# The heads of two mixers' attention passed in one row, one step apart on each engine, and queries and keys turned in banks of their own

## The reference, cut to what matters

```
h = rms_norm(x, mix_norm[l])
(na_q, na_k, na_v, df_q, df_k, df_v,
 gq_q, gq_k, gq_v, dl_q, dl_k, dl_v) = split_in_proj(h @ w_in[l])
o_a = neighborhood_attention(...)      # 4 heads of 64, with a bias
o_b = diff_attention(...)              # 4 heads, each two softmaxes of width 32, p[0] - lam*p[1]
o_c = gqa_axial_attention(...)         # 4 query heads, 2 key/value heads of 64
o_d = dilated_attention(...)           # 4 heads of 64, log-counts as a bias
o = jnp.concatenate([o_a, o_b, o_c, o_d], axis=-1)
x = x + o @ w_out[l]
```

## Time and profile before

| | |
|---|---|
| median of 3 runs | 3191.75 us (3189.97 to 3192.04) |
| the profiled execution, its time | 3195.57 us |
| the profiled execution, its span | 3193.5 us |
| PE busy | 3029.3 us, 95% of the span |
| DVE busy, ACT busy, POOL busy | 2097.6 us, 1597.0 us, 492.8 us |
| mean granted clock of PE | 0.974 |
| the chain that ended last | PE 85%, DVE 10%, ACT 3% |
| the two mixers | about 2245 to 2413 us and 2822 to 2989 us of the span |

### The profile page before, as it was taken

One profiled execution on the slowest core, in us unless ns is written; L12 is line 12 of the kernel. 1 busy time (PEld: TensorE's weight loads), 2 busy tenths in 40 slices (PEclk: granted clock), 3 DMA queues, 4 the chain that ended last, 5 costly groups with the idle time before them and its releaser, 6 DMA issues.

```text
span 3193.5 us, 56060 instructions
## 1 busy us (share of the span) xinstructions
PE 3029.3 (95%) x21820; PEld 2730.7 (86%) x21820; DVE 2097.6 (66%) x4342; ACT 1597.0 (50%) x3039; POOL 492.8 (15%) x371
## 2 busy tenths in 40 slices
PE   8989999999998989999999999799979999998899
PEld 8789999988787879999988888699768989976798
DVE  4559988799655456987879945654665455456544
ACT  5445544444555545554444455455535555553454
POOL 1213210000021112320000022222101213210121
PEclk9999999999999999999999999899989999999999
DMA  6345554444554334554445555455314556542354
GB/s 213 119 146 170 180 166 159 160 161 164 187 192 160 127 122 160 171 173 158 159 159 166 166 198 195 171 187 180 126 59 149 190 181 197 185 141 70 113 188 155
DMA packets 139512, 512.60 MB, mean 161 GB/s; under 512 B 15713, under 2 KB 16242, under 8 KB 137970
## 3 DMA queue, kind: packets, MB, share of 16 engines
q1 hardware_dynamic: 134352, 489.22, 46.6%
q10 hardware_dynamic: 4898, 19.81, 1.7%
HBM read 507.92 MB, written 1.05 MB: 159 GB/s over the span
## 4 chain that ended last, share of the span: by engine, by line
PE 85%; DVE 10%; ACT 3%; issue 1%; DMA 1%; ACTq 0%; DVEq 0%; SPq 0%
PE ps L415 84%; DVE WL L1580 2%; ACT WH L1037 1%; PE ps L419 1%; ACT BIG L1133 1%; DVE BIG L1692 1%; DVE BIG L1741 1%; DMA RAW<-in_w 0%; DVE XTl L1619 0%; DVE BIG L1655 0%; DVE H L1658 0%; DVE BIG L2025 0%; DVE BIG L1986 0%; DVE BIG L2032 0%; DVE BIG L1633 0%
## 5 line engine op out<-in xcount | busy, mean ns | idle before, releaser
L1037 ACT ACTIVATE WH<-RAW 128x512 fp32r<-128x512 f32 x1866 | 1168.5, 630 | 1193.8 <-PE ps L415 1167.1
L1580 DVE TENSOR_TENSOR WL<-RAW,WH 128x512 fp32r<-128x512 f32 x1537 | 1109.7, 725 | 868.6 <-ACT WH L1037 860.7
L415 PE MATMUL ps<-XTh,WH 128*128 128x256 f32 x3928 | 1131.6, 288 | 22.4 <-DVE XTl L1788 8.2
L415 PE MATMUL ps<-XTl,WH 128*128 128x256 f32 x3928 | 1120.6, 285 | 0.0
L415 PE MATMUL ps<-XTh,WL 128*128 128x256 f32 x3928 | 1119.9, 285 | 0.0
L2309 POOL TENSOR_TENSOR WL<-RAW,WH 128x512 fp32r<-128x512 f32 x329 | 441.3, 1341 | 2652.8 <-ACT WH L1037 2652.8
L415 PEld LDWEIGHTS ps<-XTh,WH 128*128 128x128 f32 x3928 | 762.9, 194 | 34.1 <-DVE WL L1580 14.5
L415 PEld LDWEIGHTS ps<-XTl,WH 128*128 128x128 f32 x3928 | 763.5, 194 | 3.1
L415 PEld LDWEIGHTS ps<-XTh,WL 128*128 128x128 f32 x3928 | 762.8, 194 | 0.0
L415 PE MATMUL ps<-WH,GH 128*128 128x512 f32 x1408 | 562.5, 399 | 20.0 <-DVE GL L2100 8.1
L415 PE MATMUL ps<-WL,GH 128*128 128x512 f32 x1408 | 554.0, 393 | 0.0
(11 more groups left out here) (182 smaller groups left out, 2209.3 us busy)
## 6 DMA issues: line engine op xcount, KB each, us to landing
RAW<-in_w SPq DMA_DIRECT2D x933, 512.0 KB, 3.3
BIG<-in_ln ACTq DMA_DIRECT2D x4, 1024.0 KB, 6.3
GAIN<-in_norms ACTq DMA_DIRECT2D x6, 512.0 KB, 4.1
BIG<-in_sk ACTq DMA_DIRECT2D x2, 1024.0 KB, 5.0
BIG<-in_na_bias ACTq DMA_DIRECT2D x2, 1024.0 KB, 10.2
BIG<-in_qk_gain ACTq DMA_DIRECT2D x2, 960.0 KB, 6.6
BIG<-in_memT ACTq DMA_DIRECT2D x4, 256.0 KB, 7.6
BIG<-in_xT ACTq DMA_DIRECT2D x1, 1024.0 KB, 5.5
```

The costliest lines, as they stand in the source:

```text
L415: return self.e.matmul(out, lhsT, rhs, start=start, stop=stop, skip_group_check=loose)
L1037: e.activation(wh, raw, ACT.Copy).then_inc(*c.hi.mark(j))
L1580: e.tensor_tensor(wl, raw, wh.bitcast(F32), ALU.subtract).then_inc(*c.lo_v.mark(j))
```

## The change

Three things are changed. First, the row of heads: `march` hands out, at every step, which head is new on PE and which are one, two, three and four steps old, over all 20 heads of a mixer in one row, without an end between groups; a group's head enters only when its queries, keys and values are there. On PE a step is now the turn of the head two steps old, then the scores of the new one, and after a yield the values of the head three steps old. DVE and ACT do maximum and exponentials of the head that is one step old, the copy of the turned head after the yield, and the division of the head four steps old. A step costs 1.4 + 0.9 where it cost 0.9 + 0.5 + 0.9 before. Second, one set of attention buffers serves all groups. Third, queries and keys are turned in banks 0/1 (`na`, `df`), 2/3 (`gq`) and, as before, 6/7 (`dl`), and the output pair of `na` goes to bank 0. Both memory attentions use the same row with one group.

```
+QK_BANK = {"na": 0, "df": 0, "gq": 2, "dl": 6}
-ATT_STEPS = {"scores": 0.9, "turn": 0.5, "values": 0.9}
+ATT = (1.4, 0.9)
...
-        t.att = [self.att_views(Arena(big, ar.at + 3700 * k)) for k in range(2)]
+        t.att = self.att_views(ar)
...
+def march(pace, groups):
+    ids = [(g, i) for g in groups for i in range(len(g.heads))]
+    flow, n = [None] * 4, 0
+    while n < len(ids) or any(x is not None for x in flow[-4:]):
+        enters = n < len(ids) and ids[n][0].needs <= pace.reached
+        flow.append(n if enters else None)
+        n += enters
+        at = flow[:-6:-1]
+        if all(x is None for x in at):
+            flow.pop()
+            yield None
+            continue
+        yield at
+        if at[4] is not None:
+            g, i = ids[at[4]]
+            if i == len(g.heads) - 1:
+                pace.reached.add(g.tag)
...
 class Tensor
+    def attention(self, groups, t):
+        for at in march(self.pace, groups):
+            ...
+            new, _, turn, out, _ = at
+            if turn is not None:
+                ps = self.bank(6)
+                for blk in range(2):
+                    e.wait_ge(*c.exps.at(*ids[turn], blk))
+                    ...
+                self.empty[6] = (c.probs_a if turn % 2 else c.probs_v).at(*ids[turn])
+            if new is not None:
+                h, ps = heads[new], self.bank(4 + new % 2)
+                ...
+            yield ATT[0]
+            if out is not None:
+                e.wait_ge(*(c.probs_a if out % 2 else c.probs_v).at(*ids[out]))
+                ps = self.bank(7)
+                ...
+                self.empty[7] = c.att_out.at(*ids[out])
+            yield ATT[1]
...
 class Tensor, norm
-            b = 6 + (g // 2) % 2
+            b = QK_BANK[name] + (g // 2) % 2
 class Tensor, first_out_mix
-        self.pair(stage, c.mix.O, 0, 6, [c.att_out.at((stage, "na"), 3)])
+        self.pair(stage, c.mix.O, 0, 0, [c.att_out.at((stage, "na"), 3)])
 class Tensor, Scalar and Vector, mix_stage
-        pace.bg += [self.attend(stage, name, k % 2) for k, name in enumerate(NAMES)]
+        pace.bg.append(self.attention(c.mix_groups(stage), t.att))
...
 class Scalar
+            _, n, turn, _, _ = at
+            if n is not None:
+                if n >= 3:
+                    e.wait_ge(*c.flipped.at(*ids[n - 3]))
+                e.wait_ge(*c.maxed.at(*ids[n]))
+                (two exponentials)
+            yield ATT[0]
+            if turn is not None and turn % 2:
+                (copy of the turned head)
+            yield ATT[1]
...
 class Vector
+            _, n, turn, _, done = at
+            if n is not None:
+                (bias, maximum)
+            if done is not None:
+                (division)
+            yield ATT[0]
+            if turn is not None and turn % 2 == 0:
+                (copy of the turned head)
+            yield ATT[1]
```

More of the change, by code:

```diff
@@ L318, in mem_heads, with mix_groups @@
         return heads
+    def mix_groups(self, stage):
+        return [Group((stage, name), self.mix_heads(name), [(stage, "made", name), (stage, "v", name)]) for name in NAMES]
     def mix_heads(self, name):
@@ L347, in __init__, with flat @@
         self.q, self.k, self.v, self.col, self.bias, self.minus = q, k, v, col, bias, minus
[L350 to L358, removed]
+class Group:
+    def __init__(self, tag, heads, needs=()):
+        self.tag, self.heads, self.needs = tag, heads, set(needs)
+def march(pace, groups):
[15 more added lines that the diff above has]
+                pace.reached.add(g.tag)
+def flat(groups):
+    return [h for g in groups for h in g.heads], [(g.tag, i) for g in groups for i in range(len(g.heads))]
 def top_steps(n, cost):
@@ L539, in pair @@
         self.empty[b] = c.xtl.at(stage, "o", g)
[L541 to L545, removed]
+    def attention(self, groups, t):
+        c, e = self.c, self.e
+        heads, ids = flat(groups)
+        for at in march(self.pace, groups):
+            if at is None:
+                yield 1.0
+                continue
+            new, _, turn, out, _ = at
[3 more added lines that the diff above has]
+                    e.wait_ge(*c.exps.at(*ids[turn], blk))
+                    for k in range(2):
+                        m = self.tr(ps[:, k * 256 + blk * 128:k * 256 + blk * 128 + 128],
+                                    t.E[:, turn % 3, blk * 256 + k * 128:blk * 256 + k * 128 + 128])
+                m.then_inc(*c.flipped.mark(*ids[turn]))
+                self.empty[6] = (c.probs_a if turn % 2 else c.probs_v).at(*ids[turn])
+            if new is not None:
+                if ids[new][1] == 0:
+                    self.ready(*ids[new][0])
+                h, ps = heads[new], self.bank(4 + new % 2)
@@ L2327, in inner, with attention @@
             yield cost
-    def attention(self, tag, n):
-        yield from att_steps(n)
-        self.pace.reached.add(tag)
+    def attention(self, groups):
+        for at in march(self.pace, groups):
+            if at is None:
+                yield 1.0
+                continue
+            yield ATT[0]
+            yield ATT[1]
     def states(self):
@@ L2483, in norm @@
         self.pace.reached.add((stage, "made", name))
-    def attend(self, stage, name):
-        while not {(stage, "made", name), (stage, "v", name)} <= self.pace.reached:
-            yield 1.0
-        yield from self.attention((stage, name), 8 if name == "df" else 4)
     def mix_stage(self, layer):
@@ L2496, in mix_stage @@
         pace.reached |= {(stage, "v", "na"), (stage, "v", "df")}
-        pace.bg += [self.attend(stage, name) for name in NAMES]
+        pace.bg.append(self.attention(self.c.mix_groups(stage)))
         self.halves(8)
```

195 lines of the change are left out of this document (75 added, 120 removed).

## The result

The changed kernel takes 3206.78 us (median of 6 runs, 3200.34 to 3208.52) against 3191.89 (median of 6, 3188.70 to 3194.04): 1.0045 of the time before, 95% interval 1.0032 to 1.0058. It is slower, by 14 to 15 us, where 3183 was forecast and 3194 was the top of the range.

What follows compares the result with a forecast made beforehand. PE was taken to bound the mixers: waits plus clock loss go from 28.4 to 22.8 us a mixer, less 1 for hand-overs, so 4.6 each, 9.2 for two. From the median 3191.75 that gives 3183 us, range 3171 to 3194.

Steps and rivals of the forecast that it cites:

- the hand-overs: Mixers: 1 us a mixer taken off the gain for hand-overs between engines that the step-by-step count leaves out.
- The bound and the two sums: Mixers' attention: PE bounds; 20.7 us idle and 7.9 us of clock, together 28.4 a mixer, are the most to win.
- The memory attentions: Two memory attentions, same row with one group: waits few and apart, so no effect, within 1 us each way.
- The removed waits: Mixers: nearly all of 20.5 us of PE's waits go, among them 2.87 on the pair's low part and 3.5 before the second pair.
- The added waits: Mixers: new PE waits, mostly behind norms and divisions on DVE, eight over 1.3 us, 18.8 us a mixer in all.
- the walk: Mixers: PE, DVE and ACT followed through the new order with traced durations, giving 18.8 us of waits against 20.5.
- The 0.7 us of the held operation: `gq` norm on DVE: a small operation takes 0.91 us, not 0.17, under POOL's low part; 0.7 of the 3.5 us wait.
- I take 2 each, 4 a mixer, against 7.9: Clock in the mixers: two low spells instead of three, costing 2 us each, 4 a mixer where it was 7.9.
- the prediction's own sign of being wrong: Profile after: wrong if low spells are four or more, waits on copies are small, or waits appear in feed-forward stages.
- Waits only moved: Rival, mixers: the clock still loses 7.9, so only 0.7 us a mixer is won; 3190 (3187 to 3194), chance 0.27.
- Slower: Rival, mixers: eight waits over 1.3 us, five low spells of 2.6 us, 4.4 us a mixer lost; 3200, chance 0.11.
- Wrong if waits on copies are small (then the gain is twice as large): Sign, mixers: small waits on copies would mean DVE keeps further ahead than assumed, doubling the gain.

Runs made afterwards that it cites:

- m1_mem_cost: The changed kernel, but in the two memory attentions a step charges the pace only for what it does, 9.2 in all instead of 18.4: 3197.23 us, ratio 1.0008.
- m3_banks_only: The kernel before with the bank change alone (turned queries and keys, first output pair): 3193.28 us, ratio 1.0006.
- m7_before_fill: The kernel before with 14, 9 and 20 matmuls of no use at its mixers' waits of 2.60, 1.75 and 3.55 us: 3193.00 us, ratio 0.9997.
- m14_before_act_copies: The kernel before with all copies of turned heads in the mixers on ACT: 3195.24 us, ratio 1.0010.
- m11_divide_first: The changed kernel with the memory price mended, all turned heads in the mixers copied by ACT, and DVE's division ahead of the maximum: 3196.57 us, ratio 1.0013.
- m6_fill_all: The changed kernel with the memory price mended and 19, 14, 8 and 11 matmuls of no use at PE's waits in each mixer: 3182.78 us, ratio 0.9962.

## Why the prediction was wrong, point by point

In the traces the forecast of -9.2 us became +12.1. The account in us, forecast against measured, with the clock by the windows of 2 us:

| term, whole kernel | forecast | measured | off by |
|---|---|---|---|
| two memory attentions | 0 | +9.3 | +9.3 |
| clock in the two mixers | -7.8 | +13.6 | +21.4 |
| PE's idle time in them, with the hand-overs | -1.4 | -15.3 | -13.9 |
| the rest of PE's longer work in them | 0 | +5.1 | +5.1 |
| elsewhere | 0 | -0.6 | -0.6 |

So the clock was the largest miss, and the error in the idle time hid more than half of it: that the mixers came out only 12.6 us off is luck.

**The bound and the two sums.** Right that PE bounds the mixers and that idle time and clock can be won or lost: filling the idle time on PE moved the kernel from 3197 to 3183 with its order as it was. Wrong in "no instruction is added or dropped, so the sum is one of waits": the matmuls are the same, but no two heads' scores run together any more, and PE's work grew by some 2.5 us a mixer beyond the clock. The sum had no term for that.

**The memory attentions, "I take nothing, within 1 us each way".** The first step that failed: 9.5 us by m1_mem_cost, three quarters of the 12.1 in the trace, and so most of the loss against the kernel before. I read the change's line on costs (1.4 + 0.9 for 0.9 + 0.5 + 0.9) as the same price and counted only their own waits. But the new row charges a step whole, also when it fills and drains: 4 heads take 8 steps of 2.3, 18.4 of credit, where the old one charged 9.2. All that stands behind in the same background queue came later, by some eight halves at the 1.0 to 1.2 of credit that a half gives in the GLA stage, where it met the point at which PE does all that is left in the queue. The waits that followed were at lines that no term spoke of.

**The removed waits.** Gone in the trace as said, the 2.87, the 3.55, and the back-to-back values. "Its 2.87 us go whole" and "the pair's bank 0 is free there" are right only on the new row; on the old one the pair waits 2.1 us for bank 0 (m3_banks_only). And what went with the drained and refilled row was not only waits: its back-to-back scores were PE's fast ones.

**The added waits.** Seven of the eight places were right; six sizes were too large and the first too small: 3.2, 2.4, 0.8, 1.4, 1.3, 1.8, none and 0.95 where the walk had 1.7, 3.5, 1.55, 1.65, 1.8, 2.35, 1.4 and 1.6. For the first, the walk had the norm's two operations at the lengths of `gq`, 1.01 and 0.94 us, where those of `df` take 1.28 and 1.21; that is 0.5 of the 1.5 us it was short. In sum PE waits 13.2 us in the stretch for the walk's 18.8, and idles 7.6 us less in a mixer, where the walk had 1.7. Some of the difference may itself be the clock, as PE's own work between two waits takes longer at 1.2 GHz and DVE catches up; no run separates that.

**The 0.7 us of the held operation.** It is there again: 0.90 for L1629 at 2326.00, with POOL's 1.26 us from 2325.61 over it; the two end within 0.03 us of each other. By the Trainium skill's rule ("SBUF — State Buffer", "Who interferes with whom") this is no accident, and the second trace agrees.

**The clock, "I take 2 each, 4 a mixer, against 7.9".** The second step that failed. The granted clock took 8.5 and 5.1 us more from the mixers than before, where the sum had it give 3.9 back in each. I had three reasons. Two falls instead of three: there were three in the first mixer and four in the second, as the prediction's own sign of being wrong had it. About seven us a fall: the last lasted from 2373 to 2393. And the reading of the earlier trace rows, that a single wait of 2.9 us need not bring the clock down: m7_before_fill shows the same wait bringing it down, and m14_before_act_copies shows it and one of 3.5 passing. One window at 1.00 was taken for a rule. In the attention stretch the clock took 17.1 and 13.6 us (8.5 in each before, by the same windows), and with fills it took nothing, so this term should have had a range from nothing to about twice that of before.

**The rivals.** "Waits only moved" (3190, 0.27) has the mixers' outcome but not their terms: with the memory price mended the kernel stands at 3197.2, ratio 1.0008, above that rival's 3194, and it stands there because idle time went down and the clock's loss and PE's own work went up by about as much. "Slower" (0.11) had the right sign and named the clock; its 13 us of clock loss are near the 17.1 and 13.6 of the trace, but its waits (18.8) are not, and its 3200 had nothing from the memory stages either. Extra matmuls that close PE's idle gaps made the kernel faster by 14 us, and shorter ones by 9 (3197.2 to 3182.8 and 3188.1). The rule that I weighed against the change, of short PE idles between groups of matmuls that make the clock swing (the Trainium skill, "TensorE: Matmul & The Clock Gate", "A second HAM failure mode: psum-queue depth-cycling"), agrees with that better than I had given it credit for. Which gap does it, the runs don't tell.

**"Wrong if waits on copies are small (then the gain is twice as large)".** The waits on copies were 7.9 us, for 9.9 in the walk, so the sign as such didn't come. What it priced did: PE's idle time was 5.6 us smaller than walked in the stretch, and the mixers were still no shorter.

Open: what the pairs of scores are worth; why the same wait brings the clock down in one execution and not in another; why m11_divide_first lost; and what the row of heads is worth with the old banks.

## What to carry to other kernels

When a schedule charges steps to a pace, add up the charge of everything that shares the code, also of empty steps, and look at who stands behind it in the queue. Where PE's idle gaps are short and many, a sum of waits is only half the price: count PE's busy time before and after, and give the clock a range of its own. Before you spread out work that stands back to back, look in the trace whether it runs together: eight matmuls took the time of four here. Cheap matmuls of no use in a gap can tell what the clock costs, once their bank is free at that moment and their length fits (on the kernel before only the third placing did). And a wait that ends last says little of what it is worth until the next one behind it is known, and a bank that is free in one order can be taken in another.

## What the runs showed that I had not expected

Work of no use pays: 52 extra matmuls in each mixer (12 us of PE time) brought 14 us (3197.2 to 3182.8), and 25 of them on top of ACT's copies 7.6 us (3181.7 to 3174.0). Two mixers of one execution, with the same instructions and nearly the same waits, took 179.95 and 176.45 us, and 178.6 and 172.4 in m11_divide_first: low spells start at other places. This may be why m1_mem_cost with its idle gaps spreads more (3189 to 3200) than m6_fill_all, whose clock stayed up (3182.1 to 3184.5). And the scores of two heads back to back, eight matmuls, take 1.07 us where the four of one head take 1.05, so that an order with the same matmuls can cost PE more time.
